# Expert weights read in runs of 8 KB a partition, and one of twelve lower parts of an expert made by GpSimd

## What is computed

```python
def expert_choice_moe(h, w_router, w_gate, w_up, w_down):
    xf = h.reshape(n, d)
    logits = jnp.einsum('nd,de->ne', xf, w_router).astype(jnp.float32)
    aff = jax.nn.softmax(logits, axis=-1)
    gates, idx = lax.top_k(aff.T, cap)                  # cap = 2 * 512 / 16 = 64
    xe = xf[idx]
    hid = jax.nn.silu(jnp.einsum('ecd,edf->ecf', xe, w_gate)) * jnp.einsum('ecd,edf->ecf', xe, w_up)
    ye = jnp.einsum('ecf,efd->ecd', hid, w_down) * gates[..., None].astype(h.dtype)
    y = jnp.zeros_like(xf).at[idx.reshape(-1)].add(ye.reshape(-1, d))
    return y.reshape(b, s, d)

x = x + ...                                             # attention and output projection
h2 = rms_norm(x, p['norm_ffn'])
x = x + expert_choice_moe(h2, ...)
```

## Time and profile before

| | us |
|---|---|
| median of 3 runs | 1068.93 |
| lowest and highest | 1068.01, 1069.25 |
| the profiled execution | 1068.55 |
| its span, first to last instruction | 1066.7 |

### The profile page before, as it was taken

The page is one execution under the profiler, slowest core; times in us unless marked ns, Lnnn a source line. Parts: engine busy times, 40 slices in busy tenths (PEclk is TensorE's granted clock), DMA queues, the critical chain, the costliest instruction groups (busy, mean ns, idle before and its releaser), DMA issues.

```text
span 1066.7 us, 16425 instructions
## 1 busy us (share of the span) xinstructions
PE 1021.6 (96%) x5401; PEld 867.1 (81%) x5401; DVE 889.2 (83%) x1123; ACT 771.3 (72%) x1071; POOL 495.6 (46%) x458
## 2 busy tenths in 40 slices
PE   8999998999999999995999999999999999999995
PEld 7999987888788888885778888888888777877784
DVE  6787669999999955478999999989998999889982
ACT  7655568999999834335677878778877787778772
POOL 2476479555599754444342344224432343224031
PEclk9999999999999999996999999999999999999998
DMA  8132050111332369745999999999999999999992
GB/s 310 70 125 106 1 200 11 51 32 40 110 104 67 100 172 302 223 125 173 347 362 382 388 408 390 392 389 387 409 392 390 388 408 390 392 390 398 401 372 40
DMA packets 90128, 270.30 MB, mean 253 GB/s; under 512 B 16273, under 2 KB 24684, under 8 KB 89820
## 3 DMA queue, kind: packets, MB, share of 16 engines
q1 hardware_dynamic: 84272, 252.34, 63.4%
q0 software_dynamic: 5744, 17.29, 6.6%
q10 hardware_dynamic: 60, 0.01, 0.0%
HBM read 243.27 MB, written 26.35 MB: 253 GB/s over the span
## 4 chain that ended last, share of the span: by engine, by line
DVE 15%; PE 15%; DMA 13%; issue 7%; ACT 2%; POOLq 0%; DVEq 0%; POOL 0%; SPq 0%
DMA raw<-in_w_down 12%; DVE lo L2297 11%; PE ps L2129 3%; PE ps L2130 3%; PE ps L2131 3%; ACT hi L2219 2%; PE ps L2143 1%; PE ps L2144 1%; PE ps L2145 1%; DVE h L2319 1%; DVE xelo L2308 1%; DMA out<-y,give 1%; DVE xt L2313 1%; PE ps L2106 0%; DMA xe<-h,idxT 0%
## 5 line engine op out<-in xcount | busy, mean ns | idle before, releaser
L2297 DVE TENSOR_TENSOR lo<-raw,hi 128x2048 fp32r<-128x2048 f32 x191 | 431.8, 2287 | 39.4 <-ACT hi L2219 39.2
L2219 ACT ACTIVATE hi<-raw 128x2048 fp32r<-128x2048 f32 x192 | 367.0, 1919 | 103.6 <-DMA raw<-in_w_down 51.0
L2129 PE MATMUL ps<-hi,xehi 128*128 128x512 f32 x480 | 189.0, 394 | 6.5 <-DVE xelo L2308 5.5
L2131 PE MATMUL ps<-hi,xelo 128*128 128x512 f32 x480 | 187.0, 390 | 0.0
L2130 PE MATMUL ps<-lo,xehi 128*128 128x512 f32 x480 | 186.9, 389 | 0.0
L2060 POOL COPY take<-idx 128x4 uint32 (+1 forms) x15 | 29.0, 1935 | 205.2 <-DVE xt L2313 200.5
L2065 POOL DMA_INDIRECT xe<-h,take x60 | 106.0, 1766 | 25.1 <-issue 13.7
L2129 PEld LDWEIGHTS ps<-hi,xehi 128*128 128x128 f32 x480 | 90.1, 188 | 28.3 <-DVE lo L2297 7.8
L2131 PEld LDWEIGHTS ps<-hi,xelo 128*128 128x128 f32 x480 | 90.1, 188 | 19.0
L2130 PEld LDWEIGHTS ps<-lo,xehi 128*128 128x128 f32 x480 | 90.2, 188 | 17.7
L1423 DVE TENSOR_TENSOR probTlo<-ps,probThi 128x512 fp32r<-128x512 f32 x128 | 87.6, 684 | 14.3 <-ACT probThi L1378 11.8
(11 more groups left out here) (302 smaller groups left out, 2168.7 us busy)
## 6 DMA issues: line engine op xcount, KB each, us to landing
raw<-in_w_down SPq DMA_DIRECT2D x64, 1024.0 KB, 13.1
raw<-in_w_gate SPq DMA_DIRECT2D x60, 1024.0 KB, 11.3
raw<-in_w_up SPq DMA_DIRECT2D x60, 1024.0 KB, 11.3
w_raw<-in_w_in SPq DMA_DIRECT2D x8, 592.0 KB, 8.8
x<-in_x SPq DMA_DIRECT2D x8, 512.0 KB, 4.0
r<-reciprocal_sums SPq DMA_DIRECT2D x32, 128.0 KB, 3.0
attention_out<-pj SPq DMA_DIRECT2D x16, 256.0 KB, 2.5
woraw<-in_w_o SPq DMA_DIRECT2D x4, 1024.0 KB, 5.8
```

Of the source, the lines that this page charges most:

```text
L2129: pe.matmul(ps[:, dst[n], :], rowhi[:, c, :], hi[w][:, cols], start=c == 0, stop=False)
L2131: last = pe.matmul(ps[:, dst[n], :], rowlo[:, c, :], hi[w][:, cols], start=False, stop=c == KD - 1)
L2219: act.activation(hi[s][:], raw[r][:], ACT.Copy).then_inc(hi_done, 1)
L2297: dve.tensor_tensor(lo[s][:], raw[r][:], hi[s][:].bitcast(F32), ALU.subtract).then_inc(lo_done, 1)
```

## The change

Three things are done.

First, in each chunk of gate and up, partition p now gets rows that lie next to each other: the matrix is cut into 128 groups of 8 rows, partition p has group p, and chunk i takes rows 2i and 2i + 1 of each group. A chunk of down is again 256 rows in one piece, two neighbouring rows for each partition. Both give one run of 8 KB for each partition. Expert 0's gate and up are still read in pieces of one row.

Second, all that meets these rows is put in the matching order: `h2` is written with another order of its columns (ScalarE and GpSimd now read one operand in steps of 8 elements), `gffn` is loaded in one DMA in place of four, and the transposes of `h` take every second column.

Third, VectorE leaves out chunk 11, the last chunk of each turn; GpSimd makes its lower part (`split_last`) with a semaphore of its own, `last_low`. TensorE's last chunk of a turn and SyncE's load of chunk 5 of the next one wait for that semaphore. To have a semaphore free, `route` takes three from the projection (`xr_loaded`).

```diff
 def load_chunk(sp, a, moe, raw_loaded, slot, name, e, i):
     dst = moe["raw"][slot][:].rearrange("p (k n) -> p k n", k=2)
     if isinstance(e, int) and e == 0 and name in GATE_UP:
-        rows = a[name][0].rearrange("(g l b j) n -> l b j g n", g=2, l=P // SQUARE, b=QUARTERS)
+        rows = a[name][0].rearrange("(b j k l) n -> l b j k n", b=QUARTERS, j=SQUARE, k=2)
...
-    src = a[name][bass.ds(e, 1), 2 * i * P:2 * (i + 1) * P, :].rearrange("e (k p) n -> p (e k) n", p=P)
+    if name in GATE_UP:
+        src = a[name][bass.ds(e, 1)].rearrange("e (p c) n -> p (e c) n", c=KD)[:, 2 * i:2 * i + 2, :]
+    else:
+        src = a[name][bass.ds(e, 1), 2 * i * P:2 * (i + 1) * P, :].rearrange("e (p k) n -> p (e k) n", k=2)
     sp.dma_start(dst, src).then_inc(raw_loaded[slot], 16)
...
     def sync_program(sp):                                  # route
-        for b in range(QUARTERS):
-            sp.dma_start(gffn[:, b * D // QUARTERS:(b + 1) * D // QUARTERS].rearrange("p (c j) -> p c j", j=SQUARE),
-                         a["norm_ffn"].rearrange("(c b j) -> b c j", b=QUARTERS, j=SQUARE)[b].partition_broadcast(P)).then_inc(small_loaded, 16)
+        sp.dma_start(gffn[:], a["norm_ffn"].partition_broadcast(P)).then_inc(small_loaded, 16)
...
-                pool.tensor_tensor(h2[u % 2][:], h2[u % 2][:], gffn[:], ALU.mult).then_inc(h2_done, 1)
+                rows = h2[u % 2][:].rearrange("p (b c j) -> p b c j", b=QUARTERS, j=SQUARE)
+                pool.tensor_tensor(rows, rows, gffn[:].rearrange("p (b j c) -> p b c j", b=QUARTERS, j=SQUARE), ALU.mult).then_inc(h2_done, 1)
...
-            act.activation(h2[j % 2][:].rearrange("p (b c j) -> p c b j", b=QUARTERS, j=SQUARE),
-                           x1[j % 2][:].rearrange("p (c b j) -> p c b j", b=QUARTERS, j=SQUARE), ACT.Copy, scale=r2(j)).then_inc(h2_scaled, 1)
+            act.activation(h2[j % 2][:].rearrange("p (b c j) -> p b c j", b=QUARTERS, j=SQUARE),
+                           x1[j % 2][:].rearrange("p (b j c) -> p b c j", b=QUARTERS, j=SQUARE), ACT.Copy, scale=r2(j)).then_inc(h2_scaled, 1)
...
         def load(e, j, name, of, i):                       # experts, SyncE
-            sp.reg_mov(need_split, at(e, j) - RING + 1)
-            sp.wait_ge(raw_loaded[0], 16)
-            sp.wait_ge(lo_done, need_split)
+            freed = j - RING if j >= RING else j - RING + CHUNKS
+            if freed == CHUNKS - 1:
+                sp.reg_mov(need_split, e - 1)
+                sp.wait_ge(raw_loaded[0], 16)
+                sp.wait_ge(last_low, need_split)
+            else:
+                sp.reg_mov(need_split, low_at(e, freed if j >= RING else freed - (CHUNKS - 1)) + 1)
+                sp.wait_ge(raw_loaded[0], 16)
+                sp.wait_ge(lo_done, need_split)
             load_chunk(sp, a, moe, raw_loaded, raw_of(e, j), name, of, i)
...
+        def split_last(e):                                 # experts, GpSimd
+            s, r = slot_of(e, CHUNKS - 1), raw_of(e, CHUNKS - 1)
+            pool.reg_mov(need_high, at(e, CHUNKS - 1) + 1)
+            pool.wait_ge(idx_ready, 2)
+            pool.wait_ge(hi_done, need_high)
+            pool.tensor_tensor(lo[s][:], raw[r][:], hi[s][:].bitcast(F32), ALU.subtract).then_inc(last_low, 1)
...
         with pool.Fori(2, LAST) as e:
             pool.wait_ge(xt_ready, e + 2)
             gather(e + 1)
+            split_last(e - 1)
             add_rows(e - 2)
+        split_last(LAST - 1)
         add_rows(LAST - 2)
+        split_last(LAST)
         add_rows(LAST - 1)
...
     def tensor_program(pe):
-        def transposes(src, bank, cols, ready):
+        def transposes(bank, first, ready):
             for i in range(4):
-                last = pe.transpose(ps[:, bank, i * P:(i + 1) * P], src[:, cols + i * P:cols + (i + 1) * P], k["ident"][:])
+                start = (first + i) // 2 * 2 * P + i % 2
+                last = pe.transpose(ps[:, bank, i * P:(i + 1) * P], h[:, start:start + 2 * P - 1:2], k["ident"][:])
...
-            pe.wait_ge(lo_done, at(e, j) + 1)              # down
+            if j == CHUNKS - 1:
+                pe.wait_ge(last_low, e)
+            else:
+                pe.wait_ge(lo_done, low_at(e, j) + 1)
...
-                if j + AHEAD < CHUNKS:                     # VectorE's turn
+                if j + AHEAD < CHUNKS - 1:
                     split(e, j + AHEAD)
-                elif more or j + AHEAD - CHUNKS < DOWN_CHUNKS:
+                elif j + AHEAD >= CHUNKS and (more or j + AHEAD - CHUNKS < DOWN_CHUNKS):
                     split(e + 1, j + AHEAD - CHUNKS)
```

More of the change, by code:

```diff
@@ L981, in project @@
     signals = {"rows_ready": rows_ready, "mla_ready": mla_ready, "kv_done": kv_done, "proj_done": proj_done,
-               "row_copied": row_copied, "ones_ready": ones_ready, "rows_set": rows_set, "rk_done": rk_done, "pj_stored": pj_stored, "mla_stored": mla_stored, "pj_back": pj_back, "mla_back": mla_back, "xlo_done": xlo_done, "clo_done": clo_done}
+               "row_copied": row_copied, "ones_ready": ones_ready, "rows_set": rows_set, "rk_done": rk_done, "pj_stored": pj_stored, "mla_stored": mla_stored, "pj_back": pj_back, "mla_back": mla_back, "xlo_done": xlo_done, "clo_done": clo_done, "w_loaded": w_loaded}
     return (sync_program, gpsimd_program, tensor_program, scalar_program, vector_program), signals
@@ L1455, in attend @@
                       "score_ready": score_ready, "prep_lo": prep_lo, "pt_ready": pt_ready, "wo_lo": wo_lo, "preps": len(preps),
-                      "ones_ready": ones_ready, "o_stored": o_stored, "mla_stored": project_signals["mla_stored"]}
+                      "ones_ready": ones_ready, "o_stored": o_stored, "mla_stored": project_signals["mla_stored"],
+                      "w_loaded": project_signals["w_loaded"]}
     return (sync_program, gpsimd_program, tensor_program, scalar_program, vector_program), attend_signals
@@ L1504, in route @@
     sem = phase.sem
-    xr_loaded = [sem(f"xr_loaded{i}") for i in range(3)]
+    xr_loaded, W_LOADED = attend_signals["w_loaded"][0:3], 16
     small_loaded, wr_scaled, aff_cleared = sem("small_loaded"), sem("wr_scaled"), sem("aff_cleared")
@@ L1596, in rest @@
             group_sums(1)
-            pool.wait_ge(small_loaded, 16 * (QUARTERS + 1))
+            pool.wait_ge(small_loaded, 32)
             pool.tensor_tensor(wr[:], wr[:], k["gcol"][:, G_FFN:G_FFN + KD].unsqueeze(2).to_broadcast([P, KD, EXPERTS]),
@@ L1827, in add_first @@
             dve.wait_ge(ro_done, j + 1)
-            dve.wait_ge(xr_loaded[j % 3], 16 * (j // 3 + 1))
+            dve.wait_ge(xr_loaded[j % 3], W_LOADED + 16 * (j // 3 + 1))
             for n in range(2):
@@ L1992, in experts @@
     OFFSET = GU_CHUNKS % RING
-    TAIL = GU_CHUNKS + CHUNKS * LAST
     merged, x1_stored, h2_stored, h2_done, rows_set = (
@@ L2005, in at, with low_at @@
         return j if isinstance(e, int) and e == 0 else CHUNKS * e - DOWN_CHUNKS + j
+    def low_at(e, j):
+        return j if isinstance(e, int) and e == 0 else (CHUNKS - 1) * e + (GU_CHUNKS - CHUNKS + 1 + j)
     def slot_of(e, j):
@@ L2019, in experts @@
     sem = phase.sem
-    hi_done, lo_done, chunk_used = sem("hi_done"), sem("lo_done"), sem("chunk_used")
+    hi_done, lo_done, last_low, chunk_used = sem("hi_done"), sem("lo_done"), sem("last_low_done"), sem("chunk_used")
     route_ready, gates_ready, idx_ready = sem("route_ready"), sem("gates_ready"), sem("idx_ready")
@@ L2054, in gpsimd_program @@
     def gpsimd_program(pool):
-        need_copied, need_free, need_output = (pool.alloc_register(n) for n in ("need_copied", "need_free", "need_output"))
+        need_copied, need_free, need_output, need_high = (
+            pool.alloc_register(n) for n in ("need_copied", "need_free", "need_output", "need_high"))
         def gather(e):
@@ L2137, in down @@
             w = slot_of(e, j)
-            pe.wait_ge(lo_done, at(e, j) + 1)
+            if j == CHUNKS - 1:
+                pe.wait_ge(last_low, e)
+            else:
+                pe.wait_ge(lo_done, low_at(e, j) + 1)
             for kk in range(2):
@@ L2153, in last_down @@
                     if n == 0:
-                        pe.wait_ge(lo_done, TAIL + d + 1)
+                        pe.wait_ge(lo_done, low_at(EXPERTS, d) + 1)
                         if d % 2 == 0:
@@ L2169, in turn @@
             for b in range(2):
-                transposes(h, X[b], b * BANK, ht_ready)
+                transposes(X[b], 4 * b, ht_ready)
             for i in range(1, 4):
@@ L2177, in turn @@
                 pe.wait_ge(h_done, 2 * LAST + 1)
-                transposes(h, X[0], 0, ht_ready)
+                transposes(X[0], 0, ht_ready)
             down(e, 2)
@@ L2182, in turn @@
                 pe.wait_ge(h_done, 2 * LAST + 2)
-                transposes(h, X[1], BANK, ht_ready)
+                transposes(X[1], 4, ht_ready)
         pe.wait_ge(merged, 1)
@@ L2202, in tensor_program @@
         last.then_inc(xt_ready, 1)
```

(4 more changed lines are left out.)

## The result

The changed kernel takes 1132.52 us (median, 1131.91 to 1132.77) where the kernel before takes 1069.09 beside it: 1.0592 times as long, interval 1.0578 to 1.0606. The forecast was 1106 with a range up to 1132: sign and place are as forecast, the time lies 0.5 us above the range, and the loss of 63 us is 26 us larger than the 37 of the sum.

What follows compares the result with a forecast made beforehand. Later turns were taken as paced by DMA at 34.6 us; the change's loop through the late split was summed to 37.1. Twelve turns add 33.7 us, the end 5 less 1.4: +37.3 on 1068.55, so 1106 us, range 1072 to 1132.

Steps and rivals of the forecast that it cites:

- five signs: Profile after: longer `take` spacing, DMA row down with 8 KB packets, slow split beside VectorE, late chunk 5 load, ScalarE waiting.
- T: The time at which GpSimd ends the split of a turn, forecast 14 to 15 us after chunk 4's load goes out.
- T to chunk 9 landed: SyncE's loads: first load on a dry queue 5.8 us, four more chunks 9.9, the scatter among them 1.3.
- upper part, lower part, xt: ScalarE's upper part 1.92, VectorE's lower part 2.29 and `xt` behind it 1.24: 5.4 us.
- take and gathers: GpSimd's copy and gathers before the split: 9.8 us, between 7.5 if nothing blocks them and 10.9 as before.
- wait for VectorE, and the split: GpSimd waits 0.4 us (of 0 to 2.3) for VectorE's instruction under way, then its split takes 4.5.
- 5 - 1.4 = 3.6: After the loop: TensorE's last chunk starting at T adds 5 us; two remaining turns paced by DMA save 1.4.
- The 8 KB runs: Loads of 8 KB packets: 2.48 us a chunk (2.40 to 2.54), so DMA needs 33.9 us a turn.
- (a): Rival: the loop is shorter than 33.9 us, so only the DMA gain remains: 1061 us, chance 0.13.
- (b): Rival: as (a), and 8 KB packets are no faster than 417 GB/s: 1068 us, chance 0.03.
- (c): Rival: gate and up loads lose DMA rate with runs 32 KB apart: 1113, or 1126 to 1135 us; chance 0.06.
- exclusion: GpSimd's 4.52 us split stops VectorE's lower parts and `xelo`, and itself first waits 0 to 2.3 us for VectorE.

Runs made afterwards that it cites:

- the 4 KB kernel: Kernel before with only GpSimd making chunk 11's lower part, old layout and 4 KB packets kept (also called the split alone): 1121.10 us, 1.048.
- the runs alone: Kernel before with only the new layout and runs of 8 KB; VectorE makes all twelve lower parts, nobody waits for `last_low`: 1063.44 us, 0.9935.
- the 21.1 us above: Time from split's end to `xt` in the changed kernel with chunk 11's own raw buffer and 20 unused TensorE transposes: 1096.94 us, 1.0261.
- the two signals: Changed kernel, VectorE making all lower parts; GpSimd signals after a one-element copy (1083.61 us) or after two small powers (1157.48 us).
- the own raw buffer: Changed kernel with a separate raw buffer for chunk 11, so SyncE's load of chunk 5 no longer waits for `last_low`: 1110.83 us, 1.0377.

## Why the prediction was right in kind and short in size

**The mechanism held.** The five signs that I named are there: chunk 5's load waits for T (801.61 behind 801.47), `xelo` and lower parts beside the split last over 4 us, the DMA row is down to 8 and 9 with packets of 8 KB, the turns are longer, and ScalarE waits for the loads behind T. One name was wrong: it waits for `in_w_down` (chunk 9) and `in_w_gate`, not for `in_w_up`. The landing that ends the loop is chunk 9's.

**The loop's terms**, in the turn from T = 801.47 to T = 840.91:

```
                                  forecast   measured
T to chunk 9 landed               17.0       819.11 - 801.47 = 17.6
upper part, lower part, xt        5.4        824.51 - 819.11 = 5.4
take and gathers                  9.8        835.16 - 824.51 = 10.65
wait for VectorE, and the split   4.9        840.91 - 835.16 = 5.75
sum                               37.1       39.4
```

The step that failed is the gathers' 9.8 and the split's 4.9, sized 1.7 us too low together; the loads made 0.6 more. For the gathers I took off a microsecond "since of three lower parts that lie in the way one is gone". It isn't the number of them that counts but what a gather meets: the first one is free now (1.01 in place of 2.27), the second waits for a whole lower part (2.90). In the turns where this doesn't happen they end after 9.0 us, and in the 4 KB kernel after 8.7, so a value between 8.7 and 10.7 was there to be had and couldn't be read from before. For the split I took 0.4 for the wait; 5.71 to 6.06 in all the turns against 4.52 for it alone make it 1.2 to 1.5. I had 0 to 2.3 as its ends, and chose too near the lower one. The mean of twelve turns is 38.96, 1.86 more than forecast: 12 x 1.86 = 22.3 us.

**The end.** From the last `take` to the end it is 104.2 us before (1066.7 - 962.52) and 111.5 after (1130.6 - 1019.10), 7.3 more, where I had 5 - 1.4 = 3.6. T is 1.7 later than I had, and TensorE's last chunk goes in part at half clock: it takes 4.2 us for 2.7 (from 1035.33 to the next turn's first matmul at 1039.56), 1.5 more, a term that the sum had at nothing. With them it is 6.8, and 0.5 stay unexplained. The half clock is in the row behind the last split of the loop:

```profile
1035.27:1038.20 2.93, 2.87 (x7) 2.29 (x8) 2.93 (x3) 0.00 (x0) 0.60 (x2) 0.50 0.60 190
```

Ahead of the first `take` 0.6 more are lost. 1106 + 22.3 + 3.7 + 0.6 comes to the 1132.5 measured, within 0.1. It lies half a microsecond above my range. The mean turn of 38.96 is still inside my 35.2 to 39.0, at its very end, since all the errors of its terms went one way; what carried the time over the edge is the end, for which the range left no room.

**The 8 KB runs.** I took 2.48 us a chunk. The undisturbed 429 GB/s make it 2.44, and 12 x 2.44 + 4.1 = 33.4 for DMA. The turns of the runs alone, 33.64, show that it needs no more than that, so my 33.9 was too much; TensorE ended the gain, at some 6 us of time. The rule that I weighed (the Trainium skill, DMA: Bandwidth & Descriptors, Why small descriptors are slow) gives 1.2% for 4 KB to 8 KB; the rows have 2.9% (429 against 417), and the measurement decides.

**The rivals.** (a) and (b), a loop under 33.9: the split alone is 4.8% slower, out. (c), the layout: the runs alone are faster, out; 32 KB between the runs of a load costs nothing that can be seen at 404 GB/s. What I called exclusion was right as a mechanism, with another price: at the place where the change put it, it costs only by making T later (GpSimd's side), and VectorE's blocked `xelo` lies in the wait for loads (read from the line of the two signals, not tried by itself). With SyncE released, VectorE's side stands in the path (the 21.1 us above). Whether it is the 1.0 us a turn of the split ahead of the gathers isn't shown, since ScalarE's wait for `give` is there as well. The Trainium skill (SBUF — State Buffer, SBUF: two separate sides) says that of a VectorE instruction with two SBUF inputs and a GpSimd instruction that reads SBUF the one that begins first keeps the other out until it is through. The rows agree both ways: 5.93 for GpSimd's split behind a VectorE part, 5.61 for a 1.28 us pair of VectorE's behind GpSimd.

**What I missed** is that TensorE's own wait for `last_low` makes a second loop, 1.6 us a turn shorter than SyncE's. It didn't change the time, but it is why freeing the buffer wins back only 22 of 63 us; in every second turn of that kernel the limit is a third one, VectorE with two lower parts held up by the split.

## What to carry to other kernels

When work moves to another engine, ask first when its end comes, not whether the engine has room. GpSimd had 20 idle us in a turn, and what counted was that the split stood behind 10.65 us of gathers; made ahead of them, the kernel is 6 us slower than before and not 63. Each waiting engine closes a loop of its own, so look for the second one before freeing the first. And a kernel with turns that repeat multiplies: here 1 us of lateness in a turn was 12 us of time.

## What the runs showed of the hardware

TensorE's clock, behind its wait for the late split. In the changed kernel it waited 3.8 to 5.3 us in nine turns; the granted clock fell to 0.50 (1.2 GHz), at once or within some 2 us, and the last chunk took 4.0 to 5.3 us, 4.6 in the mean. In the four turns in which it waited 1.60 us the clock stayed at 1.00 (2.4 GHz), and the chunk took 2.85. The other kernels show that the length of the wait alone doesn't settle it: behind 1.94 us (the kernel with the split only) the mean is 0.64 over 4.7 us, and behind 3.73 us (the own raw buffer, at 829.92) it once stayed at 1.00. Before the change there was no such wait (at most 0.8 us in the loop), and the clock didn't move.

```profile
908.80:913.50 4.70, 4.70 (x14) 3.70 (x15) 4.70 (x4) 1.42 (x1) 2.14 (x1) 0.64 0.74 254
...
865.46 0.50 PE L2171 MATMUL ps<-hi,hthi 128*128 128x512 f32 x1 [1.61 <-POOL lo L2086]
...
865.40:868.50 3.10, 3.04 (x13) 2.39 (x14) 3.10 (x3) 0.40 (x1) 2.21 (x2) 1.00 0.57 238
...
829.92 0.50 PE L2171 MATMUL ps<-hi,hthi 128*128 128x512 f32 x1 [3.73 <-POOL lo L2086]
...
829.90:834.00 4.10, 4.08 (x18) 3.40 (x19) 4.10 (x4) 0.94 (x2) 0.56 (x1) 1.00 0.93 388
```

The second thing is how dear small work on GpSimd is: 1.42 us for a copy of one element per partition, 2.14 for a power of 8 columns and 4.15 for 16.
